# Scores of eight differential and eight dilated heads: three single-pass products of rounded parts and remainders in place of one float32 product

## The reference, cut to what matters

```python
def diff_attention(q, k, v, lam):            # "differential" heads, two halves c of 64 columns
    s = jnp.einsum('bhcqe,bhcke->bhcqk', qblk, kt, preferred_element_type=jnp.float32) * (d ** -0.5)
    p = jax.nn.softmax(s, axis=-1)
    a = p[:, :, 0] - lam * p[:, :, 1]
    ...
def dilated_attention(q, k, v):              # "dilated" heads: three windows of one score matrix
    ...
    s = jnp.einsum('brhnqe,brhnke->brhnqk', qs, kb, preferred_element_type=jnp.float32) * (Dh ** -0.5)
    ...
```

## Time and profile before

| | us |
|---|---|
| median of three runs | 2542.74 (2542.72 to 2543.06) |
| the profiled execution's own time | 2542.45 |
| its span, first to last instruction | 2540.7 |
| granted clock of PE, mean over the span | 1.000 of full speed |

### The profile page before, as it was taken

How to read it: one execution, slowest core, us unless ns; L and a number is a source line. 1 busy time by engine, 2 the same in 40 slices (tenths; PEclk the granted TensorE clock), 3 DMA queues, 4 the chain that set the end, 5 groups by cost and what they waited for, 6 DMA issues and landing times.

```text
span 2540.7 us, 33424 instructions
## 1 busy us (share of the span) xinstructions
PE 2533.9 (100%) x11596; PEld 2099.3 (83%) x11596; DVE 1413.6 (56%) x1707; ACT 1229.0 (48%) x1698; POOL 138.8 (5%) x211
## 2 busy tenths in 40 slices
PE   9999999999999999999999999999999999999999
PEld 7888888888888888888888888888888888888887
DVE  5555555555555555555455555565566646665665
ACT  6555445444344434455444544544555445553553
POOL 2222200000000000000000111100000000000000
PEclk9999999999999999999999999999999999999999
DMA  8555556665666566666666666655666566666665
GB/s 239 161 171 161 169 173 185 191 189 189 193 190 189 190 192 190 191 198 190 179 185 179 182 185 179 184 176 189 184 182 190 190 192 187 178 193 195 184 189 166
DMA packets 327827, 471.16 MB, mean 185 GB/s; under 512 B 23232, under 2 KB 126244, under 8 KB 327584
## 3 DMA queue, kind: packets, MB, share of 16 engines
q1 hardware_dynamic: 326352, 467.30, 61.3%
q0 software_dynamic: 1088, 2.07, 0.3%
q10 hardware_dynamic: 272, 0.26, 0.0%
HBM read 467.44 MB, written 2.11 MB: 185 GB/s over the span
## 4 chain that ended last, share of the span: by engine, by line
PE 99%; DMA 0%; SPq 0%; DVE 0%; ACT 0%; issue 0%
PE ps L473 32%; PE ps L475 32%; PE ps L474 31%; PE ps L922 1%; PE ps L722 1%; PE ps L567 0%; PE ps L549 0%; PE ps L582 0%; PE ps L555 0%; PE ps L756 0%; PE ps L639 0%; PE ps L659 0%; PE ps L888 0%; DMA raw<-in_w_in 0%; PE ps L592 0%; PE ps L863 0%
## 5 line engine op out<-in xcount | busy, mean ns | idle before, releaser
L1395 DVE TENSOR_TENSOR w_lo<-raw,w_hi 128x1024 fp32r<-128x1024 f32 x880 | 1081.1, 1230 | 1078.6 <-ACT w_hi L976 1076.5
L976 ACT ACTIVATE w_hi<-raw 128x1024 fp32r<-128x1024 f32 x880 | 931.3, 1060 | 1182.3 <-PE ps L475 1172.9
L473 PE MATMUL ps<-w_hi,xT_hi 128*128 128x512 f32 x2204 | 873.3, 396 | 0.5 <-DVE xT_lo L1414 0.5
L475 PE MATMUL ps<-w_hi,xT_lo 128*128 128x512 f32 x2204 | 859.8, 390 | 0.0
L474 PE MATMUL ps<-w_lo,xT_hi 128*128 128x512 f32 x2204 | 858.3, 389 | 0.0
L473 PE MATMUL ps<-w_hi,yT_hi 128*128 128x512 f32 x1312 | 515.2, 393 | 0.0
L475 PE MATMUL ps<-w_hi,yT_lo 128*128 128x512 f32 x1312 | 511.2, 390 | 0.0
L474 PE MATMUL ps<-w_lo,yT_hi 128*128 128x512 f32 x1312 | 510.6, 389 | 0.0
L475 PEld LDWEIGHTS ps<-w_hi,xT_lo 128*128 128x128 f32 x2204 | 413.7, 188 | 87.2
L473 PEld LDWEIGHTS ps<-w_hi,xT_hi 128*128 128x128 f32 x2204 | 414.0, 188 | 85.9 <-issue 2.7
L474 PEld LDWEIGHTS ps<-w_lo,xT_hi 128*128 128x128 f32 x2204 | 414.2, 188 | 82.9
(11 more groups left out here) (204 smaller groups left out, 899.7 us busy)
## 6 DMA issues: line engine op xcount, KB each, us to landing
raw<-in_w_up SPq DMA_DIRECT2D x264, 512.0 KB, 3.7
raw<-in_w_down SPq DMA_DIRECT2D x176, 512.0 KB, 3.8
raw<-in_w_in SPq DMA_DIRECT2D x160, 512.0 KB, 3.8
raw<-in_w_gate SPq DMA_DIRECT2D x88, 512.0 KB, 3.7
raw<-in_w_out SPq DMA_DIRECT2D x60, 512.0 KB, 3.7
raw<-in_w_in SPq DMA_DIRECT2D x128, 192.0 KB, 2.8
raw<-in_w_in SPq DMA_DIRECT2D x192, 128.0 KB, 2.5
raw<-in_w_proj_m SPq DMA_DIRECT2D x16, 512.0 KB, 3.8
```

Source lines behind the costliest of these rows:

```text
L473: pe.matmul(o, hi[:, q], w_hi[n % NS][:, k, 0:width], start=first, stop=False)
L475: mm = pe.matmul(o, lo[:, q], w_hi[n % NS][:, k, 0:width], start=False, stop=last)
L976: nc.scalar.activation(w_hi[n % NS][:, :, 0:width], raw[n % NS][:, :, 0:width], ACT.Copy).then_inc(hi_ready, 1)
L1395: v.tensor_tensor(w_lo[n % NS][:, :, 0:width], raw[n % NS][:, :, 0:width], f32(w_hi[n % NS][:, :, 0:width]), ALU.subtract).then_inc(lo_rea ...
```

## The change

Queries and keys of differential and dilated heads are no longer copied to `qkT` but rounded to float32r, into tiles 6 (queries) and 7 (keys) of `yT_hi`. DVE subtracts these from the bank of transposes and leaves the remainders in the same tiles of `yT_lo`: two instructions of 256 columns for a differential head, as its queries are scaled, one of 512 for a dilated head. A new semaphore, `qk_lo`, tells of them, and PE waits for it where it waited for `qkT`. Each float32 matmul of the scores becomes three float32r matmuls into the same sum. On DVE the new piece stands at unit 0 of the head, in `diff_head` and `dil_head`, behind the split of that unit's weights and behind whatever the head before does at that unit. ACT's two instructions stay, with another destination. The mLSTM and fox heads have no such semaphore and keep the float32 path.

```diff
--- before.py
+++ after.py
@@ -166,6 +166,7 @@
         self.rope = one("rope")
         self.qk_T = one("qk_T")
         self.qkT = one("qkT")
+        self.qk_lo = one("qk_lo")
         self.scores = one("scores")
         self.masked = one("masked")
         self.raw_max = one("raw_max")
@@ -240,6 +241,7 @@
         rows_kept = nc.dram_tensor("key_rows", (HEADS + M_HEADS, S), F32, kind="Internal").ap()
         gz, lf, f_sum = sb("gz", [NT, NG]), sb("lf", [NT, NG]), sb("f_sum", [NT, NG])
         gt, key_bias = sb("gt", [NT, NG]), sb("key_bias", [NT, HEADS + M_HEADS])
+        q_part, k_part = slice(6 * S, 7 * S), slice(7 * S, 8 * S)
         gates_T = y[0:2 * NG, 0, :]
         rows_out = y[0:HEADS + M_HEADS, 1, :]
         biased = prob[:, 2 * S:2 * S + 3 * P]
@@ -305,8 +307,8 @@
         stored, half_done = sem("stored"), sem("half_done")
         hb = HeadSems(sem, "diff", ("masked", "raw_max", "v_staged"))
         ha = HeadSems(sem, "dil", ("raw_max", "coef", "sq", "ms", "rstd", "y", "y_T"))
-        hm = HeadSems(sem, "mlstm", ("rope", "v_staged"))
-        hf = HeadSems(sem, "fox", ("rope", "row_max", "coef", "y", "y_T"))
+        hm = HeadSems(sem, "mlstm", ("rope", "v_staged", "qk_lo"))
+        hf = HeadSems(sem, "fox", ("rope", "row_max", "coef", "y", "y_T", "qk_lo"))
 
         block = ctx.enter_context(nc.Block())
         ds = bass.ds
@@ -626,18 +628,25 @@
             pe.wait_ge(gain_ready, 1)
 
 
+            def scores(o, rows, t, first, last, a_part, b_part):
+
+                return pe.matmul(o[:, t * S:(t + 1) * S], a_part[rows, q_part.start + t * P:q_part.start + (t + 1) * P],
+                                 b_part[rows, k_part], start=first, stop=last)
+
             def diff_head(u, h):
 
                 u_qk, u_scores, u_p, u_values, u_y = HEAD_STEPS
                 if u == u_qk:
                     turn_qk(hb, h)
                 if u == u_scores:
-                    pe.wait_ge(hb.qkT, h.upto(2))
+                    pe.wait_ge(hb.qk_lo, h.upto(2))
                     for t in range(NT):
                         for c in range(2):
-                            e = slice(c * 64, (c + 1) * 64)
-                            mm = pe.matmul(ps[5 + c][:, t * S:(t + 1) * S], qkT[e, 0, t * P:(t + 1) * P], qkT[e, 1, :],
-                                           start=True, stop=True)
+                            scores(ps[5 + c], slice(c * 64, (c + 1) * 64), t, True, False, yT_hi, yT_hi)
+                        for c in range(2):
+                            scores(ps[5 + c], slice(c * 64, (c + 1) * 64), t, False, False, yT_hi, yT_lo)
+                        for c in range(2):
+                            mm = scores(ps[5 + c], slice(c * 64, (c + 1) * 64), t, False, True, yT_lo, yT_hi)
                             if t == NT - 1:
                                 mm.then_inc(hb.scores, 1)
                 if u == u_p:
@@ -654,10 +663,11 @@
                 if u == u_qk:
                     turn_qk(ha, h)
                 if u == u_scores:
-                    pe.wait_ge(ha.qkT, h.upto(2))
+                    pe.wait_ge(ha.qk_lo, h.upto())
                     for t in range(NT):
-                        mm = pe.matmul(ps[5][:, t * S:(t + 1) * S], qkT[:, 0, t * P:(t + 1) * P], qkT[:, 1, :],
-                                       start=True, stop=True)
+                        scores(ps[5], slice(0, P), t, True, False, yT_hi, yT_hi)
+                        scores(ps[5], slice(0, P), t, False, False, yT_hi, yT_lo)
+                        mm = scores(ps[5], slice(0, P), t, False, True, yT_lo, yT_hi)
                     mm.then_inc(ha.scores, 1)
                 if u == u_p:
                     pe.wait_ge(ha.mixed, h.upto(2))
@@ -1020,9 +1030,10 @@
 
 
             def qk_out(s, h, scale):
+                q, k = (yT_hi[:, q_part], yT_hi[:, k_part]) if s.qk_lo else (qkT[:, 0, :], qkT[:, 1, :])
                 act.wait_ge(s.qk_T, h.num(1, FREE + 1))
-                nc.scalar.activation(qkT[:, 0, :], ps[4][:, 0:S], ACT.Copy, scale=scale).then_inc(s.qkT, 1)
-                nc.scalar.activation(qkT[:, 1, :], ps[4][:, S:2 * S], ACT.Copy).then_inc(s.qkT, 1)
+                nc.scalar.activation(q, ps[4][:, 0:S], ACT.Copy, scale=scale).then_inc(s.qkT, 1)
+                nc.scalar.activation(k, ps[4][:, S:2 * S], ACT.Copy).then_inc(s.qkT, 1)
 
             def p_out(s, h, n):
                 act.wait_ge(s.p_T, h.upto())
@@ -1472,7 +1483,11 @@
 
             def diff_head(u, h):
 
-                _, u_scores, _, _, u_y = HEAD_STEPS
+                u_qk, u_scores, _, _, u_y = HEAD_STEPS
+                if u == u_qk:
+                    dve.wait_ge(hb.qkT, h.upto(2))
+                    v.scalar_tensor_tensor(yT_lo[:, q_part], ps[4][:, 0:S], B_SCALE, f32(yT_hi[:, q_part]), ALU.mult, ALU.subtract).then_inc(hb.qk_lo, 1)
+                    v.tensor_tensor(yT_lo[:, k_part], ps[4][:, S:2 * S], f32(yT_hi[:, k_part]), ALU.subtract).then_inc(hb.qk_lo, 1)
                 if u == u_scores:
                     for c in range(2):
                         dve.wait_ge(hb.scores, h.upto(2, c + 1))
@@ -1496,7 +1511,11 @@
                     y_lo(hb, h, ps[7], S, HEADS, 1, lambda e: gain[:, G_SUBLN:G_SUBLN + 1])
 
             def dil_head(u, h):
-                _, u_scores, _, _, u_y = HEAD_STEPS
+                u_qk, u_scores, _, _, u_y = HEAD_STEPS
+                if u == u_qk:
+                    dve.wait_ge(ha.qkT, h.upto(2))
+                    both = slice(q_part.start, k_part.stop)
+                    v.tensor_tensor(yT_lo[:, both], ps[4][:], f32(yT_hi[:, both]), ALU.subtract).then_inc(ha.qk_lo, 1)
                 if u == u_scores:
                     dve.wait_ge(ha.scores, h.upto())
                     v.scalar_tensor_tensor(mix[:], ps[5][:], HEAD_SCALE, ln_count[:], ALU.mult, ALU.add).then_inc(ha.masked, 1)
```

## The result

The changed kernel takes 2548.64 us in the median of 13 runs (2548.35 to 2548.98), the kernel before, on the same chip, 2542.88 us (2542.70 to 2543.36). The ratio is 1.0022, with a 95% interval of 1.0014 to 1.0031: slower by 5.76 us. Forecast were 2548.5 us and +5.75 us.

What follows compares the result with a forecast made beforehand. PE was taken to bound the kernel, with 99% of the chain that ended last. Waits of 8.40 us less savings of 2.65 gave +5.75 us on the profiled 2542.45, 2548.5 us as the median; range 2545.0 to 2554.5.

Steps and rivals of the forecast that it cites:

- The bound: Stage of the heads: PE has 99% of the chain that ended last, so its microseconds are the whole's.
- PE's own work: Scores on PE: three float32r passes save 0.17 us in each of 16 heads, 2.65 us less in all.
- The steps of 0.117 us: PE's gate matmuls, float32r with 256 columns, begin 0.117 us apart; the score passes were forecast at that pace.
- The halves paired: Differential scores: twelve matmuls pair into six steps; rival 1, no pairing, 5.6 us more, 2554.1 us, chance 0.08.
- The rule on weight loads: Dilated scores: loads overlap matmuls only on different rows; as rival 2, 5.2 us more, 2553.7 us, chance 0.03.
- DVE's lateness: Unit 0 of heads: PE waits for DVE's subtractions behind the split and the scaling, 8.40 us more in all.
- The unseen instruction without a factor: DVE's subtraction without a factor at 128x256, not in the trace: taken as 0.415 us, bounds 0.35 and 0.68.
- What stands behind the subtractions: DVE after the subtractions: no weight split, load of `raw` or row maxima is late; no time added.
- The other side: Rival 3, DVE at unit 0: DVE is not late, only the 2.65 us savings are left, 2540.1 us; chance 0.14.
- Rival 3: DVE not late at unit 0: none to half of the waits, 2540.1 to 2544.3 us; chance 0.14.

Runs made afterwards that it cites:

- the experiment that has the wait alone: Against the kernel before: scores stay float32 from `qkT`, but DVE makes the subtractions and PE waits for them without using them; 2551.09 us, ratio 1.0034.

## Why the prediction was right

**The bound.** PE's line was the right one to count on: the changes of the slots, +5.94 us, are the change of the time, +5.76, to within the 0.4 us by which starts differ. That +5.75 was forecast and +5.76 measured is closer than the working was: by the slots the savings are 0.13 us smaller and the waits 0.06 larger than forecast, so +5.94, and that the last 0.2 us vanished in the medians is luck.

**PE's own work.** Forecast 2.65 us less; the sixteen slots without a wait sum to 2.52 less. The steps of 0.117 us, read from the gates, hold to 0.003 us for 128 columns of weights and for 64 rows: 0.119 and 0.120 in the changed kernel. The differential block lasted 0.91 us instead of 0.89. The halves paired.

**The rule on weight loads**, weighed against the values: in the dilated heads every load after the first lay beside a matmul on the same 128 rows. Two loads of dilated head 1:

```profile
234.68 0.19 PEld L633 LDWEIGHTS ps<-yT_hi,yT_lo 128*128 128x128 f32 x1
234.80 0.19 PEld L633 LDWEIGHTS ps<-yT_hi 128*128 128x128 f32 x1
```

The first starts with the matmul listed at 234.68 and so lies beside it, and the matmuls follow each other at 0.12 us (five steps from 234.68 to 235.28), with no room for 0.11 us more each. The trace does not agree with the rule, as the prediction gives it, of the Trainium skill ("TensorE: Matmul & The Clock Gate", Part 3: Packing small matmuls — row/col tiling); the measurement decides.

**DVE's lateness.** Forecast 8.40 us; 8.46 by the slots, 8.5 in the experiment that has the wait alone. Head by head the slots were 1.01 (heads 1, 2, 5), 0.74 (3, 4, 7) and 1.26 us (6) longer than the 1.56 without a wait, against 0.98 to 1.01, 0.74 and 1.26 by the prediction's working; dilated head 0 lost 0.87 (0.86 forecast), the seven others 0.15 each, as forecast. The unseen instruction without a factor took 0.416 us against the 0.415 taken.

**What stands behind the subtractions.** No split and no unit was late, as the order of starts had said; the experiments with more and with less ahead of the split agree.

**The other side.** Rival 3 named 0.72 us as the point that decides. Moving the subtractions ahead on DVE crosses it, and the time falls to 2540.10 us; the forecast for that case was 2540.1. The fall below the kernel before is 2.45 us on that chip, where 2.65 was forecast; that the two times agree to the tenth is luck.

## What to carry to other kernels

Work moved to an engine that is half idle still costs the bound engine's time if it stands at the wrong place in that engine's order: read from the timeline when the instruction ahead of it ends and when its reader arrives. A new piece that the bound engine waits for belongs ahead of work that is needed only units later. Three single-pass matmuls in place of one float32 matmul pay where the moving side is long enough to hide a weight load, here at 256 columns (0.35 against 0.43 us) and not at 128 (0.28 against 0.22).

## What the hardware showed beyond what was expected

Two streams of matmuls on different 64 rows need not alternate in the program to run side by side: with three of one half written ahead of three of the other, each pair still started within 0.01 us. So the description of the engines in the first section, each running its own list in order, does not hold for the starts of PE's matmuls on different rows. With six written ahead, the other half started three early and the rest ran alone. How far a half can run ahead with other lengths or loads was not tried.
